# Hybrid decoder step on one core: the prompt's mask and softmax division moved to TensorE, five digit counts to ScalarE

## The chip, the cores and the metric

The kernel runs on one core of a Trainium2 chip. The metric is the device time of one execution in microseconds (us). The trace is one profiled execution; the engines are named TensorE (PE; PEld is its weight load), VectorE (DVE), ScalarE (ACT), GpSimd (POOL) and SyncE (SP).

## What is computed

Two layers of a decoder trunk for 256 prompt positions and 8 sample sequences (264 columns together), in float32. Each layer is a gated feed-forward part, a mixer, and a second feed-forward part:

```python
def layer(x, ...):
    h = macaron_ffn(x, ffn1)                       # x + 0.5 * rmsnorm(swiglu(rmsnorm(x)))
    y, state = token_mixing(rmsnorm(h), ...)       # w_in -> [conv | pool | sparse attention] -> w_out
    h = h + rmsnorm(y)
    return macaron_ffn(h, ffn2)

def dsa_prompt(q, k, v, qi, ki, wi, pos):          # 8 heads of 64, 2 key heads, blocks of 128 queries
    sc = indexer_scores(qi, wi, ki)                # sum over 4 index heads of relu(qi . ki) * wi
    sc = where(pos_k <= pos_q, sc, -inf)
    _, sel = top_k(sc, 64)                         # the 64 best keys of each prompt query
    return softmax over sel of (q . k) / 8, times v

def dsa_sample(...):                               # the same over 1024 cached keys and the new one,
    _, sel = top_k(sc, 256)                        # the 256 best of 1025; keys and values by page table
```

## The kernel before

**Feed-forward and units.** Weights come in units of 128 x 1024 floats, loaded by SyncE into six slots of `raw`. Most units are split into a high part (`w_hi`, by ScalarE, line 380) and a rest (`w_lo`, by VectorE, line 601), and each product is three fp32r products (`three`, lines 1111 to 1113). The mixer's units 9 to 15 are used unsplit, as fp32 products of eight pieces (`whole`, line 1219).

**The mixer, first stretch.** The input projection has 15 units (`unit`, then `whole`). VectorE scales each and turns queries and keys (`turned`, `rope_end`). The prompt's 64 best keys are found by eight rounds of `top8` (line 757): MAX8 and MATCH_REPLACE8 on `wk1` (256 columns) and `wk0` (128), which write TAKEN over what was found. Three rounds stand before the key unit, one after it, two after count 6 and two after count 7. The samples' 256th score is found as eight digits of a threshold: `count(i)` compares Z (16 trial values times 8 sequences on 128 partitions, 1025 columns) with the trial value and sums the flags (line 792), tests the sum against the rank (line 793), and signals `count`; TensorE sums the tests over the partitions of a sequence (`digit`, line 1237) into PSUM bank 6; `digit(i)` on VectorE makes the next trial value (lines 807 to 811). TensorE's order is: digit 0, unit 11, digit 1, unit 12, digit 2, unit 13, digit 3, unit 14, digit 4, `taps(0, 2)`, digit 5, `taps(2, 3)`, digit 6, `taps(5, 3)`, digit 7. The taps are the convolution: 496 matmul instructions of 32 x 32 weights per layer (line 1249) into banks 3, 4, 5 and 7.

**Second stretch.** ScalarE copies the taps' sums to `cpart` (line 497), TensorE folds them (line 1260). The sample keys (`keys(0)`, `keys(1)`, line 1363) use four slots of `kv`; the second batch of 32 transfers is issued by SyncE (line 264) when `keys(0)` has freed them. The prompt's attention runs over four pairs of heads j, with two buffers. `scores(j)` (lines 1377, 1378) writes banks 2 and 3; `masked(j)` on VectorE adds the mask into `sp_` (line 923), takes the maximum of each half (lines 925, 926) and scales it (line 928); `exps(j)` on ScalarE makes four exponentials with sums (line 510); `norm(j)` on VectorE takes the reciprocal (line 932) and multiplies `sp_` (line 935); TensorE transposes both halves, one into bank 7 and one into bank 0 (line 1419); ScalarE copies them to `pT` (line 528); TensorE multiplies by the values (lines 1435, 1436), ScalarE and VectorE split the result (lines 541, 956). In ScalarE's order `exps(j+1)` stands before the copies of pair j. In TensorE's order the loop body is: both transposes of j, `scores(j+2)` (for j < 2) or `keys(1)` (j = 2) or `new_key` (j = 3), values of j. The convolution's centring and variance use bank 6. After the loop the samples' mask, maximum and exponential follow (lines 1026 to 1030, 544).

**Third stretch.** TensorE transposes the samples' probabilities (line 1451), multiplies by the cached values (`values`, line 1481), does two output pieces (`out_part(1)`, `out_part(2)`), transposes the sample result (line 1491), multiplies the pool's averages (line 1495), and then waits for their split (lines 557, 1054) before the other output pieces (lines 1111 to 1113).

The order of each engine is the order in which its block is written; semaphores tie the engines together.

## Time and profile before

| | us |
|---|---|
| three runs | 1138.27, 1145.15, 1140.99 (median 1140.99) |
| profiled execution: its own time | 1138.1 |
| its span (first to last instruction) | 1136.4 |
| mixer of layer 0, from first unit to output projection | about 212 to 350 |
| mixer of layer 1 | about 770 to 908 |
| mean granted TensorE clock | 0.988 |

The page gives the busy time of each engine. The chain of work that ended last follows releases back from the end; each of its rows is a start, a duration and what ran. A timeline row has start, duration, engine, line, operation, output <- input with shapes, the number of instructions merged into it, and in brackets how long the engine had been idle and what ended that. An fp32 product appears as two instructions.

### The profile page before, as it was taken

What the parts mean: (1) busy time and instruction counts of PE and PEld (TensorE: products, weight loads), DVE (VectorE), ACT (ScalarE), POOL (GpSimd) and SP (SyncE); (2) the same over time, 40 slices, a digit from 0 to 9 for tenths busy, and PEclk for the clock granted to TensorE, in tenths of its full rate; (3) what the DMA queues carried; (4) which work ended last, traced back from release to release, by engine and by line L of the source; (5) the groups of instructions that cost most, each with busy time, mean ns of one, the idle gap of its engine ahead of it and who ended that gap; (6) DMA issues with size and microseconds to landing.
All of it is one profiled execution on the core that took longest, in us unless ns stands there. A gap on an engine that the chain in (4) does not pass through costs nothing.

```text
span 1136.4 us, 27658 instructions
## 1 busy us (share of the span) xinstructions
PE 1078.3 (95%) x9374; PEld 1024.2 (90%) x9374; DVE 740.0 (65%) x1211; ACT 513.5 (45%) x830; POOL 190.0 (17%) x241
## 2 busy tenths in 40 slices
PE   6999999999779999999999999999987899999996
PEld 5999999988459999999999999998873799999995
DVE  5667744688975766764476666448889466777544
ACT  5544443631454644443464444345216455444432
POOL 4211100411311311110042111004212022111001
PEclk9999999999899999999999999999998999999998
DMA  8464565443536455555435465563345445555541
GB/s 282 163 229 150 220 210 195 162 142 107 152 97 203 134 183 183 185 185 178 155 112 193 176 232 179 198 245 122 114 139 143 100 154 190 179 181 184 185 148 39
DMA packets 90464, 191.17 MB, mean 168 GB/s; under 512 B 12322, under 2 KB 48482, under 8 KB 90402
## 3 DMA queue, kind: packets, MB, share of 16 engines
q1 hardware_dynamic: 87426, 184.82, 48.7%
q0 software_dynamic: 2976, 5.53, 2.1%
q8 instruction: 38, 0.62, 0.2%
q14 instruction: 24, 0.20, 0.1%
HBM read 187.71 MB, written 2.59 MB: 167 GB/s over the span
## 4 chain that ended last, share of the span: by engine, by line
PE 85%; DVE 6%; ACT 4%; issue 2%; SPq 1%; DMA 1%; POOL 0%; DVEq 0%; POOLq 0%; ACTq 0%
PE PS L1111 24%; PE PS L1112 23%; PE PS L1113 23%; PE PS L1219 4%; PE PS L1147 2%; PE PS L1249 2%; DVE w_lo L601 1%; SPq L264 1%; PE PS L1158 1%; PE PS L1159 1%; PE PS L1162 1%; DVE rstd_post L630 1%; ACT w_hi L380 1%; PE PS L1225 1%; PE PS L1481 1%
## 5 line engine op out<-in xcount | busy, mean ns | idle before, releaser
L601 DVE TENSOR_TENSOR w_lo<-raw,w_hi 128x1024 fp32r<-128x1024 f32 x295 | 394.6, 1338 | 307.9 <-ACT w_hi L380 305.4
L380 ACT ACTIVATE w_hi<-raw 128x1024 fp32r<-128x1024 f32 x295 | 310.7, 1055 | 250.7 <-PE PS L1113 209.9
L1111 PE MATMUL PS<-x_hi,w_hi 128*128 128x264 f32 x1456 | 415.7, 286 | 0.7 <-DVE w_lo L601 0.6
L1112 PE MATMUL PS<-x_lo,w_hi 128*128 128x264 f32 x1456 | 412.6, 283 | 0.0
L1113 PE MATMUL PS<-x_hi,w_lo 128*128 128x264 f32 x1456 | 412.3, 283 | 0.0
L1111 PEld LDWEIGHTS PS<-x_hi,w_hi 128*128 128x128 f32 x1456 | 274.2, 188 | 2.3 <-DVE w_lo L601 1.6
L1112 PEld LDWEIGHTS PS<-x_lo,w_hi 128*128 128x128 f32 x1456 | 274.4, 188 | 0.1
L1113 PEld LDWEIGHTS PS<-x_hi,w_lo 128*128 128x128 f32 x1456 | 273.0, 188 | 0.0
L1111 PE MATMUL PS<-h_hi,w_hi 128*128 (+1 forms) x832 | 237.2, 285 | 3.7 <-DVE h_lo L1054 3.7
L1113 PE MATMUL PS<-h_hi,w_lo 128*128 (+1 forms) x832 | 236.9, 285 | 0.0
L1112 PE MATMUL PS<-h_lo,w_hi 128*128 (+1 forms) x832 | 236.2, 284 | 0.0
L1111 PEld LDWEIGHTS PS<-h_hi,w_hi 128*128 128x128 f32 x832 | 156.5, 188 | 5.0 <-DVE h_lo L1054 4.6
L1112 PEld LDWEIGHTS PS<-h_lo,w_hi 128*128 128x128 f32 x832 | 157.0, 189 | 0.0
L1113 PEld LDWEIGHTS PS<-h_hi,w_lo 128*128 128x128 f32 x832 | 156.6, 188 | 0.0
L1524 POOL TENSOR_TENSOR us<-gs,us 128x264 f32<-128x264 f32 x88 | 79.9, 908 | 431.0 <-DVE us L665 401.3
L427 ACT ACTIVATE gs<-gs 128x264 f32<-128x264 f32 x88 | 37.3, 424 | 194.2 <-DVE gs L659 194.2
L1537 POOL TENSOR_TENSOR h<-h,y 128x264 f32<-128x264 f32 x45 | 38.8, 893 | 328.4 <-DVE y L645 260.4
L1219 PE MATMUL PS<-x_all,raw 128*128 128x264 f32 x192 | 45.4, 389 | 0.0
L659 DVE TENSOR_TENSOR gs<-PS,rstd 128x264 f32<-128x264 f32 x88 | 37.9, 430 | 9.4 <-PE PS L1113 5.7
L1147 PE MATMUL PS<-sq,con 128*128 128x264 f32 x96 | 30.6, 402 | 11.9 <-ACT sq L579 10.2
L1219 PEld LDWEIGHTS PS<-x_all,raw 128*128 128x128 f32 x192 | 35.7, 190 | 5.6
L673 DVE TENSOR_TENSOR h_lo<-us,h_hi 128x264 f32 x88 | 37.5, 426 | 0.0
(255 smaller groups left out, 994.8 us busy)
## 6 DMA issues: line engine op xcount, KB each, us to landing
raw<-in_wts SPq DMA_DIRECT2D x312, 512.0 KB, 3.7
kv<-in_kT SPq DMA_DIRECT2D x128, 64.0 KB, 2.0
kx<-in_kxT SPq DMA_DIRECT2D x128, 32.0 KB, 2.1
vx<-in_vC POOLq DMA_DIRECT2D x48, 64.0 KB, 2.3
raw<-in_vC SPq DMA_DIRECT2D x32, 64.0 KB, 2.3
kv<-in_vC SPq DMA_DIRECT2D x32, 64.0 KB, 2.0
out_yT<-h SPq DMA_DIRECT2D x8, 132.0 KB, 1.8
vx<-in_vC SPq DMA_DIRECT2D x16, 64.0 KB, 1.8
```

What stands on the lines that cost most here:

```text
L380: act.activation(w_hi[:, u % SPLIT, :], raw[:, u % RAW, :], ACT.Copy) \
L427: act.activation(gs[:, f % 3, :], gs[:, f % 3, :], ACT.Silu).then_inc(sem["silu"], 1)
L601: tt(w_lo[:, u % SPLIT, :], raw[:, u % RAW, :], w_hi[:, u % SPLIT, :].bitcast(F32), AL.subtract) \
L659: tt(gs[:, f % 3, :], PS[:, 2 * (f % 3), 0:NT], rstd[:, :], AL.mult).then_inc(sem["gs"], 1)
L673: tt(out, us[:, f % 3, :], hi.bitcast(F32), AL.subtract).then_inc(sem["h_lo"], 1)
L1111: pe.matmul(out, w_hi[:, w, cols], hi, start=start, stop=False)
L1112: pe.matmul(out, w_hi[:, w, cols], lo, start=False, stop=False)
L1113: return pe.matmul(out, w_lo[:, w, cols], hi, start=False, stop=stop)
L1147: pe.matmul(PS[:, 7, 0:NT], ones, sq[:, ORDER[i], :], start=(i == 0), stop=(i == KD - 1)).then_inc(sem["mm_pre"], 1)
L1219: ins = pe.matmul(PS[:, m % 2, 0:NT], raw[:, (u0 + m) % RAW, col(k)], x_all[:, k, :], start=(k == 0), stop=(k == KD - 1))
L1524: pool.tensor_tensor(us[:, f % 3, :], gs[:, f % 3, :], us[:, f % 3, :], AL.mult).then_inc(sem["mid"], 1)
L1537: pool.tensor_tensor(h[:, d, :], h[:, d, :], y[:, d, :], AL.add).then_inc(sem["h_new"], 1)
```

## The change

- `scores(j)` first writes a mask into PSUM: `hide` (minus 1e30 on the diagonal, fp32r) times `bias` (0, 1 or 2 per query and key), one product of 384 columns for each half; the score products accumulate on it. Even pairs use banks 2 and 3, odd pairs banks 6 and 7. TensorE now waits for the mask (`mask_p`) before `scores(0)`, and for `p_exp(j-1)` before `scores(2)` and `scores(3)`.
- `masked(j)` on VectorE only takes the two maxima, from PSUM, and scales them. `exps(j)` reads PSUM and writes `sp_`.
- `norm(j)` makes `share`: the identity times the reciprocals, 128 x 4 x 128; the transposes of a half become fp32 products with `share`. Both halves use bank 0, so the second waits for ScalarE's copy of the first. The freed bank 7 and bank 6 go to the scores; fold, centring and variance move to bank 1, and the values of pair 0 wait for `c_rms`.
- Digits 0 to 4: VectorE only compares; ScalarE sums 1025 flags with an accumulating copy and tests the sum with two Relu operations on one column, each behind a semaphore wait on the one before.
- TensorE's digits 0 to 3 stand in the middle of units 11 to 14, digit 4 after `taps(0, 2)`, digit 5 after `taps(2, 3)`, and digits 6 and 7 after `taps(5, 3)`.
- Three rounds of `top8` move ahead, behind counts 0, 1 and 2; one stays behind count 6, none behind count 7.
- ScalarE's splits of units 16 to 18 stand around the sum of count 4.
- In the third stretch the pool's product and the small transposes come before `out_part(1)` and `out_part(2)`.

```diff
@@ -169,6 +172,7 @@
         ties = place("ties", [128, NS], F32, [s2[0]])
+        share = place("share", [128, 4, 128], F32, [s2[0] + 4128])
         relu = place("relu", [128, 4, 256], F32, s2)
@@ -188,7 +192,7 @@
         radi = place("radi", [128, 4 + len(SHIFTS)], I32)
-        bias = place("bias", [128, 384], F32)
+        bias = place("bias", [128, 384], F32R)
         bias1, bias0 = bias[:, 0:256], bias[:, 256:384]
@@ -212,6 +216,7 @@
         spread = place("spread", [128, 128], F32)
+        hide = place("hide", [128, 128], F32R)
@@ -235,6 +240,7 @@
         CONV_BANKS = (3, 4, 5, 7)
+        SCORES = (2, 6)
@@ -479,13 +485,31 @@
+                def summed(i):
+                    act.wait_ge(sem["beyond"], at_layer(L, "beyond", i + 1))
+                    act.activation(ties[:, :], ties[:, :], ACT.Copy, accum_out=rad[:, 6:7]).then_inc(sem["total"], 1)
+                    act.wait_ge(sem["total"], at_layer(L, "total", 2 * i + 1))
+                    act.activation(rad[:, 7:8], rad[:, 6:7], ACT.Relu, scale=-1.0, bias=rad[:, 3:4]) \
+                        .then_inc(sem["total"], 1)
+                    act.wait_ge(sem["total"], at_layer(L, "total", 2 * i + 2))
+                    act.activation(rad[:, 1:2], rad[:, 7:8], ACT.Relu, scale=-1.0, bias=con[:, C_ONE:C_ONE + 1]) \
+                        .then_inc(sem["count"], 1)
+                summed(0)
                 act.wait_ge(sem["conv_r"], at_layer(L, "conv_r", 1))
...
                 ins.then_inc(sem["conv_s"], 1)
-                for m in range(16, 19):
-                    split(L, u0 + m)
+                summed(1)
+                summed(2)
+                summed(3)
+                split(L, u0 + 16)
+                summed(4)
+                split(L, u0 + 17)
+                split(L, u0 + 18)
@@ -498,16 +522,18 @@
                 for c in range(2):
-                    ins = act.activation(cacc[:, c, 0:NP], PS[:, 7, NP * c:NP * c + NP], ACT.Identity,
+                    ins = act.activation(cacc[:, c, 0:NP], PS[:, 1, NP * c:NP * c + NP], ACT.Identity,
                                          bias=pars[:, DWB + c:DWB + c + 1])
...
                     act.wait_ge(sem["s_masked"], at_layer(L, "s_masked", j + 1))
+                    if j >= 2:
+                        act.wait_ge(sem["p_t"], at_layer(L, "p_t", 2 * j - 2))
                     for a in range(2):
                         for b, (lo, hi) in enumerate(((0, 256), (256, 384))):
-                            t = sp_[:, j % 2, a, lo:hi]
-                            ins = act.activation(t, t, ACT.Exp, scale=SCALE,
+                            ins = act.activation(sp_[:, j % 2, a, lo:hi], PS[:, SCORES[j % 2] + a, lo:hi], ACT.Exp,
+                                                 scale=SCALE,
                                                  bias=spm[:, j % 2, 2 * a + b:2 * a + b + 1],
@@ -789,8 +815,11 @@
                     at_least = trial if i else radi[:, 0:1]
-                    linked(ts(ties[:, :], Z[:, :], at_least.bitcast(F32), 0.0, AL.is_ge, AL.add, accum_out=cnt))
-                    tt(reach, cnt, rank, AL.is_ge).then_inc(sem["count"], 1)
+                    if i < SUMMED:
+                        ts(ties[:, :], Z[:, :], at_least.bitcast(F32), None, AL.is_ge).then_inc(sem["beyond"], 1)
+                    else:
+                        linked(ts(ties[:, :], Z[:, :], at_least.bitcast(F32), 0.0, AL.is_ge, AL.add, accum_out=cnt))
+                        tt(reach, cnt, rank, AL.is_ge).then_inc(sem["count"], 1)
                     if i == len(SHIFTS) - 1:
@@ -873,14 +902,17 @@
                 p0 = count(0)
+                top8()
                 turned(10, aq[:, 1, :])
                 p1 = count(1)
+                top8()
                 turned(11, aq[:, 2, :])
                 p2 = count(2)
+                top8()
                 turned(12, aq[:, 3, :])
@@ -905,23 +937,15 @@
                 top8()
-                top8()
                 p7 = count(7)
-                top8()
-                top8()
                 stt(bias1[:, :], wk1[:, :], TAKEN / 2, nc01[:, 0:256], AL.is_gt, AL.add)
-                after(L, step(L, stt(bias0[:, :], wk0[:, :], TAKEN / 2, nc01[:, 256:384], AL.is_gt, AL.add)))
+                stt(bias0[:, :], wk0[:, :], TAKEN / 2, nc01[:, 256:384], AL.is_gt, AL.add).then_inc(sem["mask_p"], 1)
                     dve.wait_ge(sem["s_p"], at_layer(L, "s_p", j + 1))
-                    if j >= 2:
-                        dve.wait_ge(sem["p_t"], at_layer(L, "p_t", 2 * j - 2))
-                    s = sp_[:, j % 2, :, :]
-                    linked(stt(s, bias[:, :].unsqueeze(1).to_broadcast([128, 2, 384]), -BIG, PS[:, 2:4, 0:384],
-                               AL.mult, AL.add))
+                    s = PS[:, SCORES[j % 2]:SCORES[j % 2] + 2, :]
                     dve.tensor_reduce(spm[:, j % 2, 0:4:2], s[:, :, 0:256], AX.X, AL.max)
@@ -930,10 +954,11 @@
                     after(L, step(L, dve.reciprocal(sps[:, j % 2, :], sps[:, j % 2, :])))
-                    for b, (lo, hi) in enumerate(((0, 256), (256, 384))):
-                        t = sp_[:, j % 2, :, lo:hi]
-                        ins = tt(t, t, sps[:, j % 2, b:4:2].unsqueeze(2).to_broadcast([128, 2, hi - lo]), AL.mult)
-                    ins.then_inc(sem["p_norm"], 1)
+                    if j:
+                        dve.wait_ge(sem["p_t"], at_layer(L, "p_t", 2 * j))
+                    tt(share[:, :, :], ident.unsqueeze(1).to_broadcast([128, 4, 128]),
+                       sps[:, j % 2, :].unsqueeze(2).to_broadcast([128, 4, 128]), AL.mult).then_inc(sem["p_norm"], 1)
@@ -1210,12 +1236,14 @@
-                def whole(m):
+                def whole(m, middle=None):
...
                     for k in range(KD):
+                        if k == KD // 2 and middle is not None:
+                            digit(middle)
                         ins = pe.matmul(PS[:, m % 2, 0:NT], raw[:, (u0 + m) % RAW, col(k)], x_all[:, k, :],
@@ -1326,26 +1354,22 @@
                 pe.wait_ge(sem["v_nat"], at_layer(L, "v_nat", 1))
-                digit(0)
-                whole(11)
+                whole(11, middle=0)
                 pe.wait_ge(sem["rope"], at_layer(L, "rope", 5))
                 turned(10)
-                digit(1)
-                whole(12)
+                whole(12, middle=1)
                 pe.wait_ge(sem["rope"], at_layer(L, "rope", 6))
                 turned(11)
-                digit(2)
-                whole(13)
+                whole(13, middle=2)
                 pe.wait_ge(sem["rope"], at_layer(L, "rope", 7))
                 turned(12)
-                digit(3)
-                whole(14)
+                whole(14, middle=3)
+                taps(0, 2)
                 digit(4)
-                taps(0, 2)
+                taps(2, 3)
                 digit(5)
-                taps(2, 3)
+                taps(5, 3)
                 digit(6)
-                taps(5, 3)
                 digit(7)
@@ -1369,20 +1393,26 @@
                         pe.wait_ge(sem["rope"], at_layer(L, "rope", 8))
+                        pe.wait_ge(sem["mask_p"], at_layer(L, "mask_p", 1))
                         pe.wait_ge(sem["c_part"], at_layer(L, "c_part", 1))
+                    elif j == 1:
+                        pe.wait_ge(sem["s_masked"], at_layer(L, "s_masked", 1))
+                        pe.wait_ge(sem["c_part"], at_layer(L, "c_part", 4))
+                        pe.wait_ge(sem["v_nat"], at_layer(L, "v_nat", 1))
                     else:
-                        pe.wait_ge(sem["s_masked"], at_layer(L, "s_masked", j))
+                        pe.wait_ge(sem["p_exp"], at_layer(L, "p_exp", j - 1))
                     for a in range(2):
                         rows = slice(64 * a, 64 * a + 64)
-                        pe.matmul(PS[:, 2 + a, 0:256], aq[rows, j, 128:256], ak[rows, 0:256], start=True, stop=True)
-                        ins = pe.matmul(PS[:, 2 + a, 256:384], aq[rows, j, 0:128], ak[rows, 0:128],
-                                        start=True, stop=True)
+                        out = PS[:, SCORES[j % 2] + a, 0:384]
+                        pe.matmul(out, hide[:, :], bias[:, :], start=True, stop=False)
+                        pe.matmul(out[:, 0:256], aq[rows, j, 128:256], ak[rows, 0:256], start=False, stop=False)
+                        ins = pe.matmul(out[:, 256:384], aq[rows, j, 0:128], ak[rows, 0:128], start=False, stop=True)
                     ins.then_inc(sem["s_p"], 1)
...
                     for c in range(2):
-                        ins = pe.matmul(PS[:, 6, 0:NT], ones, t[:, c, :], start=(c == 0), stop=(c == 1))
+                        ins = pe.matmul(PS[:, 1, 0:NT], ones, t[:, c, :], start=(c == 0), stop=(c == 1))
                     ins.then_inc(sem[name], 1)
@@ -1399,24 +1429,19 @@
                 pe.wait_ge(sem["conv_s"], at_layer(L, "conv_s", 1))
-                pe.wait_ge(sem["v_nat"], at_layer(L, "v_nat", 1))
                 channel_sum(cacc, "c_sum")
...
                     for a in range(2):
-                        if j:
-                            pe.wait_ge(sem["p_tc"], at_layer(L, "p_tc", 2 * j - 1 + a))
-                        elif a == 0:
-                            pe.wait_ge(sem["conv_p"], at_layer(L, "conv_p", 1))
+                        if j or a:
+                            pe.wait_ge(sem["p_tc"], at_layer(L, "p_tc", 2 * j + a))
                         else:
                             pe.wait_ge(sem["chunk"], at_layer(L, "chunk", 15))
-                        p = sp_[:, j % 2, a, :]
                         for n, c in enumerate((256, 0, 128)):
-                            ins = pe.transpose(PS[:, (7, 0)[a], 128 * n:128 * n + 128], p[:, c:c + 128], ident)
+                            ins = pe.matmul(PS[:, 0, 128 * n:128 * n + 128], sp_[:, j % 2, a, c:c + 128],
+                                            share[:, 2 * a + c // 256, :], start=True, stop=True)
                         ins.then_inc(sem["p_t"], 1)
@@ -1484,16 +1511,16 @@
                 values(1)
-                out_part(1, (0, 1))
-                out_part(2, (0, 1))
+                pe.wait_ge(sem["pool_y"], at_layer(L, "pool_y", 1))
+                for c in range(2):
+                    ins = pe.matmul(PS[:, 4 + c, 0:NT], raw[:, w, col(4 + c)], pw[:, c, :], start=True, stop=True)
+                ins.then_inc(sem["unit_done"], 1)
                 pe.wait_ge(sem["o_sc"], at_layer(L, "o_sc", 1))
                 ins.then_inc(sem["o_st"], 1)
-                pe.wait_ge(sem["pool_y"], at_layer(L, "pool_y", 1))
-                for c in range(2):
-                    ins = pe.matmul(PS[:, 4 + c, 0:NT], raw[:, w, col(4 + c)], pw[:, c, :], start=True, stop=True)
-                ins.then_inc(sem["unit_done"], 1)
+                out_part(1, (0, 1))
+                out_part(2, (0, 1))
```

Left out of the diff: the new semaphores' counts, and the same renaming of bank 6 or 7 to bank 1 in the fold, the centring, the channel sums and the square root.

## Rows read from the trace of the kernel before

**Rows 1.** The page, part 1: busy time and share of each engine.

```profile
PE 1078.3 (95%) x9374; PEld 1024.2 (90%) x9374; DVE 740.0 (65%) x1211; ACT 513.5 (45%) x830; POOL 190.0 (17%) x241
```

**Rows 2.** Layer 0, taps: chain that ended last (start, us, what); timeline (start, us)

```profile
272.45 3.67 PE PS L1219 x16
...
276.68 3.67 PE PS L1219 x16
...
280.34 0.12 PE PS L1237 x2
...
280.46 2.69 PE PS L1249 x115
...
287.66 0.31 PE PS L1237 x2
...
289.76 4.07 PE L1249 MATMUL PS<-gp,dgw 32*32 32x256 f32 x128 [1.78 <-issue]
```

**Rows 3.** Same chain, second stretch of the mixer, layer 0

```profile
295.42 2.07 ACT cpart L497 x4
...
298.61 1.72 PE PS L1363 x16
...
301.24 0.97 DVE sp__109 L923
...
326.48 1.14 ACT psm L544 x2
```

**Rows 4.** Same chain, and timeline of VectorE, output stretch, layer 0

```profile
331.44 3.63 PE PS L1481 x128
...
332.76 0.71 DVE L1004 TENSOR_TENSOR pw<-pw,xp 128x528 f32<-128x528 f32 x1
...
336.95 0.91 PE PS L1495 x4
...
339.71 0.39 PE PS L1111
```

**Rows 5.** Timeline of SyncE and TensorE around the second keys, both layers.

```profile
300.33 17.22 SPq L264 DMA_DIRECT2D kv<-in_kT  x32
...
319.11 1.92 PE L1363 MATMUL PS<-kv,LA 128*32 128x512 f32 x16 [1.81 <-DMA kv<-in_kT]
...
877.16 3.64 PE L1363 MATMUL PS<-kv,LA 128*32 128x512 f32 x16 [1.98 <-DMA kv<-in_kT]
```

**Rows 6.** Timeline of VectorE, digit 6 and count 7 in layer 1.

```profile
848.88 0.16 DVE L807 TENSOR_SCALAR radi<-PS 128x1 int32<-128x1 f32 x1 [0.20 <-PE PS L1237]
...
850.59 0.16 DVE L793 TENSOR_TENSOR rad<-rad 128x1 f32<-128x1 f32 x1
```

**Rows 7.** Timeline of VectorE, a selection round and a comparison in layer 0.

```profile
287.20 0.61 DVE L760 MAX8 best<-wk 128x8 f32<-128x256 f32 x2
...
305.19 0.74 DVE L945 TENSOR_SCALAR equal<-X,rad 128x1025 f32<-128x1025 f32 x1
```

**Rows 8.** Timeline of the three engines in the attention loop of layer 0.

```profile
300.25 0.71 PE L1377 MATMUL PS<-ak,aq 64*128 64x256 f32 x4
...
302.23 0.69 DVE L925 TENSOR_REDUCE spm<-sp__109 128x2 f32<-128x512 f32 x1
...
310.08 1.28 ACT L510 ACT_TABLE_LOAD   x1
...
311.53 0.51 ACT L510 ACTIVATE sp__109<-sp__109,spm 128x256 f32<-128x256 f32 x1 [0.17 <-DVE spm L928]
...
313.30 0.84 ACT L528 ACTIVATE pT<-PS 128x384 f32<-128x384 f32 x2
...
328.70 2.00 PE L1451 MATMUL PS<-spread,psm 128*128 128x128 f32 x16
```

**Rows 9.** Busy time and granted clock (PEclk) in stretches of 2 us

```profile
core 0: us, PE busy (x) PEld busy (x) DVE busy (x) ACT busy (x) POOL busy (x), PEclk, DMA share, GB/s
...
878.00:880.00 2.00, 2.00 (x16) 0.45 (x8) 1.97 (x7) 1.97 (x4) 0.00 (x0) 0.50 0.43 123
```

More of the change, by code:

```diff
@@ L72 @@
 WARM = 9
+SUMMED = 5
 BIG = 1e30
@@ L91 @@
     pool_y=1, pl_ohi=1, pl_olo=1,
-    h_last=3, step=400,
+    h_last=3, step=400, beyond=SUMMED, total=2 * SUMMED,
 )
@@ L962, in centred @@
                     for c in range(2):
-                        ins = stt(cacc[:, c, :], PS[:, 6, 0:NT], -1.0 / 256, cacc[:, c, :], AL.mult, AL.add)
+                        ins = stt(cacc[:, c, :], PS[:, 1, 0:NT], -1.0 / 256, cacc[:, c, :], AL.mult, AL.add)
                     ins.then_inc(sem["c_cent"], 1)
@@ L1088, in _ @@
             dve.wait_ge(tables, 48)
+            ts(hide[:, :], ident, -BIG, None, AL.mult)
             ts(nc01[:, 0:256], con[:, C_CA1:C_CA1 + 256], -1 / BIG, None, AL.mult)
@@ L1259, in fold @@
                     for i in range(4):
-                        ins = pe.matmul(PS[32 * i:32 * i + 32, 7, :], stack[:, :], cpart[:, i, :],
+                        ins = pe.matmul(PS[32 * i:32 * i + 32, 1, :], stack[:, :], cpart[:, i, :],
                                         start=True, stop=True)
@@ L1431, in mixer @@
                         pe.wait_ge(sem["o_lo"], at_layer(L, "o_lo", j))
+                    else:
+                        pe.wait_ge(sem["c_rms"], at_layer(L, "c_rms", 1))
                     for a in range(2):
```

4 lines of the change are left out of this document (2 added, 2 removed).

## The prediction

> **What bounds the kernel now.** I read the page first, then the chain of work that ended last, then the timelines of the mixer of both layers. TensorE is busy 95% of the span [rows 1], and the chain of work follows it through units, taps and keys [rows 2, 3]. The feed-forward parts are not touched by the change, so only the two mixers can move the time. Each has three stretches. In the first, eight digits of a threshold are found beside four weight units and the convolution's taps; TensorE is never kept waiting by a digit there, and what stops it is an "issue" gap of 1.78 us in layer 0 [rows 2], after which 128 tap instructions take 4.07 us. In the second, from ScalarE's copies of the taps to the exponentials of the samples, TensorE is sparse and the chain hops between VectorE and ScalarE (from 295.42 to 326.48 us [rows 3]); there the mask and maximum on VectorE stand in the chain. In the third, the values and the output projection, TensorE stops once more, from 337.86 us (336.95 + 0.91) to 339.71 us [rows 4].
>
> The second stretch has another bound under the first one. After the first keys, SyncE issues 32 transfers in 17.22 us, and the second keys start only when they land: keys(0) at 298.61, keys(1) at 319.11 in layer 0, 20.5 us later [rows 3, 5], with 1.81 us of waiting for a DMA. In layer 1 keys(1) begins at 877.16. Whatever VectorE saves between the two key products is therefore capped.
>
> **Part 1: five digits summed by ScalarE, each a half step later.** A count on VectorE (compare with sum, then the test) takes 1.7 us from row to row (848.88 to 850.59, with the 0.4 us of the digit's own arithmetic in it [rows 6]). A plain comparison of the same width takes 0.74 us, the sum on ScalarE is bounded by its pass over 1025 columns at 1.14 us, and two operations on one column follow, 0.3 us each as an estimate (bounds 0.2 and 0.5) [rows 3, 7]. So the five results come about 0.8 us later than today. Their step of 4.23 us (272.45 to 276.68, a unit of 3.67 us and small products [rows 2]) is set by TensorE, and the digit now waits in the middle of the unit, 1.8 us later. VectorE has in each such step: digit 0.4, comparison 0.75, prefix 0.3, one selection round of 1.5 (0.61 us for its two MAX8 [rows 7], the rest replacement), and three passes of 264 columns for the turned query and its rope, 1.05 as an estimate from 0.97 for 768 columns [rows 3]: 4.0 of 4.23 us. It fits. I cost part 1 at nothing; its cover is TensorE's unit, and if VectorE were 0.3 us longer per step, four steps would cost 1 us a layer. ScalarE was idle then; its later splits for units 17 and 18 have several us of room.
>
> **Part 2: the last digits lose their cover.** Today digit 6 stands before the last three rounds of taps and digit 7 after them, so count 7 runs under the taps. Now digits 6 and 7 both stand behind the taps. From digit 6's product to the end of the test VectorE needs 1.87 us (848.88 to 850.75 [rows 6]), then the two mask writes over 384 columns, 0.6 us by the 0.97 for 768, and only then may scores(0) start, because the mask is now an operand of TensorE. In layer 0: taps end 295.4, VectorE starts 295.8, mask ready 298.3, scores(0) 298.4, where it starts at about 296.2 today, after the first of the four copies that begin at 295.42 [rows 3]. That is +2.2 us. Behind scores(0) on TensorE are queued the fold, keys(0) and so the whole series of 32 transfers. What hid the three late selection rounds was the same stretch of taps, so moving them gains nothing.
>
> **Part 3: scores with the mask added in PSUM.** Today a pair of scores takes 0.99 us from TensorE's start to VectorE's (300.25 to 301.24 [rows 3, 8]); the two halves use 64 rows each and partly overlap. A mask product of all 128 rows between them adds two of about 0.17 us and ends the overlap. Bounds: 1.3 us (overlap kept) and 2.2 us (none, and a switch each time); I take 1.8, near the middle, since four products of 0.32 us in sequence and two of 0.17 give 1.6 plus 0.2 of latency. A full-array product among 32-row taps costs 0.31 us where one among full-array products costs 0.12 [rows 2], so a switch of tile shape has a price. The Trainium skill, TensorEngine Tiling (Array Packing), Key Properties, says that changing the tiling mode drains TensorE; by that rule the figure would be 2.0 to 2.2 us, and the two digit rows agree with it. The fold waits today for the end of the copies, 297.49; now with 298.4 plus 1.62 us it starts at 300.0: keys(0) comes 2.46 us later, at 301.07, and with it everything behind. VectorE's masking pass (0.97 us [rows 3]) is gone; its two reductions and the scaling stay, 1.25 us (0.69 for the first, of two times 256 columns [rows 8], 0.35 for the second of half the width, 0.2 for the scaling).
>
> **Part 4: the loop over the four pairs of heads.** Time from keys(0) is called k. VectorE is relieved by 1.0 us per mask and 0.35 us per division. But its relief is soon used up: before exps(2) ScalarE loads a table from 310.08 to 311.36 and starts the exponentials at 311.53 [rows 8], so VectorE was the later one by 0.17 us. And two things grow. The three transposes of a half become three fp32 products: 16 such pieces take 2.00 us [rows 8], so 0.69 us for three plus 0.2 of latency, about double. Both halves now share PSUM bank 0, so the second half waits for ScalarE's copy (0.42 to 0.47 us) of the first, and in ScalarE's order that copy stands behind exps(j+1), 1.77 us (311.53 to 313.30 [rows 8]). Two such half products, one copy and one longer pair of scores stand before exps(2), partly beside VectorE's and ScalarE's other work: I take 0.6 us (bounds -0.15, what the table load leaves, and +1.5), so exps(2) starts at k+13.5 (today k+12.9). Then one turn is: exponentials 1.77, copy 0.47, second half 0.7, scores 1.62 plus 0.2, maximum 1.25, hops 0.05: 6.05 us, so exps(3) starts at k+19.6, ends at 21.4, copy and second half bring keys(1) to k+22.6. That is past the transfers (20.5): the new chain replaces the DMA as the bound, and keys(1) is 2.1 us later relative to k. Behind it: keys 1.84, values 0.8, first half 0.9, copy 0.45, second half 0.7, new key 0.45 (values and new key estimated by the speed of the keys), then the sample's mask and maximum as today, which gives the sample's exponential at k+30.8. Today it is at 326.48, so k+27.9 in layer 0; in layer 1 it is k+29.3, because there keys(1) took 3.64 instead of 1.92 us, at a granted clock of 0.50 [rows 5, 9]. So +3.0 and +1.6 us.
>
> **Part 5: output pieces moved.** The values end at 335.07 (331.44 + 3.63), the pool's product of 0.91 us starts at 336.95 today and would start there [rows 4]. It comes 1.88 us earlier; the two output pieces (12 products of 0.12 us) and the small transposes fill the wait of ScalarE and VectorE, 1.8 us. TensorE resumes at 337.95 instead of 339.71: -1.7 us a layer. The pool's averages are ready at 333.47 (332.76 + 0.71 [rows 4]), 1.6 us before they would be wanted.
>
> **Part 6: the clock.** The new loop leaves TensorE idle for some 3.4 us before the second half of turn 1, 2.3 before that of turn 2, and 2.0 after digit 6. Today three gaps of 1.8 to 2.0 us give both answers: the taps after 1.78 us [rows 2] and keys(1) of layer 1 after 1.98 us ran slow, keys(1) of layer 0 after 1.81 us at full speed [rows 5, 9]. At half speed (1.2 instead of 2.4 GHz) the pieces behind those gaps cost up to 2.3, 2.5 and 3.4 us more: 0 to 8.2 us a layer. I take 2.5, since it holds in part of the cases and for part of each piece. The Trainium skill, TensorE: Matmul & The Clock Gate, Part 4: PE-mode transpose, says transposes don't count as activity for the clock. By that rule real products in their place would hold it better, and the sum would be without these 2.5. Rows here show transposes at full clock only.
>
> **Sum**, against the profiled execution (1138.1 us, span 1136.4): part 2 and 3 +2.46 twice = +4.9; part 4 +3.0 +1.6 = +4.6; part 5 -1.7 twice = -3.4; that is +6.1 with the clock held; part 6 +5: +11, so 1149. The median of the three runs (1141.0) is 2.9 us above the profiled one; on it, 1152.
>
> **Rivals.** (a) The same chain with the clock held at the second halves, through denser work: +6.1, so 1147. For it: keys(1) of layer 0. (b) The relief pays: ScalarE's copies and the shared bank turn out cheap (second half ready within 0.5 us of the first) and scores cost 1.3. Then keys(1) is again set by the transfers, at k+20.5; the samples' exponential comes 2.1 us earlier than in (a) per layer, and three scores give 1.5 more: 6.1 - 4.2 - 3.0 = -1.1, so 1140, no change. It decides when exps(2), one turn, the last exponentials, copy and second half, which I count as 22.6 us from keys(0), fall under 20.5. Against it: the program order on ScalarE. (c) The other side: the tap stretch loses its "issue" gap and the slow taps after it (1.78, and 4.07 for 128 instructions against 3.0 at the 2.69 for 115 of the earlier taps, with 0.3 more on the last 45: 3.1 us a layer [rows 2]), because digits no longer stand at the same points. With (a) that is +6.1 - 6.2, no change; with (b) it is -7, so 1134, faster. For it: the gap moved by some 30 instructions between layers; against: nothing waited for is removed there. (d) The clock falls at every gap: +6.1 + 16, so 1163. (e) Digits come late by VectorE's full step: +2 on any case.
>
> **Chances.** Forecast with part of the clock lost 0.40; (a) 0.25; (b) 0.15; (c) 0.10; (d) with (e) 0.10. About 0.5% (5.7 us) is what a measurement of this kernel can tell from no change. Slower: the forecast 0.40, half of (a) 0.12, (d) 0.10, so 0.62. Same: the rest of (a) 0.13, two thirds of (b) 0.10, half of (c) 0.05, so 0.28. Faster: 0.05 each of (b) and (c), 0.10. The range 1139 to 1162 leaves out most of (c) and the end of (d).
>
> **What would show it.** Right: a gap of about 2 us on TensorE between digits 6 and 7; keys(0) 2.5 us after its old distance from the taps; TensorE waiting for ScalarE's copy before each second half; keys(1) waiting for no DMA; TensorE resuming the output 1.7 us sooner after the values; small rows at double length where the clock is 0.5. Wrong: a wait for kv before keys(1) as today (b), a shorter tap stretch (c), or TensorE waiting in the middle of a unit for a digit (e).

## The result, and the profile after

The changed kernel takes 1169.14 us (median of four runs, 1161.18 to 1170.69) where the kernel before, on the same chip, takes 1143.07: the ratio is 1.023, with an interval of 1.019 to 1.027. It is slower by 26 us, more than twice the 11 us that were forecast, and outside the range. The profiled execution took 1170.7 us with a span of 1169.0, so 32.6 us more span than before. The mean granted clock fell from 0.988 to 0.972.

From the page: busy time of the engines, then the granted TensorE clock in the 40 slices of the span.

```profile
PE 1116.0 (95%) x9438; PEld 1048.3 (90%) x9438; DVE 724.0 (62%) x1176; ACT 529.8 (45%) x870; POOL 190.9 (16%) x241
...
PEclk9999999999779999999999999999997899999998
```

TensorE is busy 38 us longer than in [rows 1], with only 64 more instructions. The two dips, 77 and 78, are the second stretches of the two mixers.

The chain that ended last, layer 0 (start, duration, what ran), answers to [rows 3]:

```profile
296.81 0.17 DVE rad L822
296.99 0.04 issue
297.03 0.52 PE PS L1265 x2
297.55 0.14 issue
297.68 0.66 PE PS L1407
298.34 1.15 PE PS L1408 x2
...
302.11 1.86 PE PS L1288 x8
303.97 3.41 PE PS L1387 x16
307.38 0.39 PE PS L1407
307.77 0.63 PE PS L1408 x2
308.40 0.22 PE PS L1409 x2
...
326.00 1.15 PE PS L1408 x2
...
335.38 3.21 PE PS L1387 x16
...
345.15 1.14 ACT psm L570 x2
```

The digit's product (L1265) waits for VectorE's test, then comes the first pair of scores (mask L1407, scores L1408 and L1409), the fold and keys(0), and keys(1) only at 335.38. Two numbers carry the case. A score product of 256 columns takes 0.63 us at 307.77 and 1.15 us at 298.34 and 326.00. Keys take 3.41 and 3.21 us, against 1.72 in [rows 3]. The granted clock says why (stretches of 2 us: start:end, length, busy time of PE, PEld, DVE, ACT and POOL, then PEclk, DMA share, GB/s):

```profile
298.00:300.00 2.00, 2.00 (x6) 1.31 (x5) 0.01 (x1) 0.00 (x0) 0.57 (x2) 0.50 0.59 172
...
308.00:310.00 2.00, 2.00 (x10) 1.46 (x9) 0.13 (x1) 0.00 (x0) 0.82 (x2) 1.00 0.60 167
...
328.00:330.00 2.00, 2.00 (x7) 1.47 (x8) 0.20 (x1) 0.00 (x0) 0.00 (x0) 0.50 0.44 124
...
334.00:336.00 2.00, 2.00 (x10) 1.28 (x14) 0.52 (x1) 0.57 (x2) 0.00 (x0) 0.50 0.00 0
```

TensorE is busy without a gap in all four, and in three of them it runs at 1.2 GHz. I summed the time at the lower level from such rows over both mixers (a stretch at 0.75 counts as half of its length): 20.5 us before, 58.0 us after. The waits ahead of the falls are in TensorE's waits and timeline of the changed kernel (waits: line waited for, total, times, longest; timeline as before, idle time and its end in brackets):

```profile
PE PS L1443 <- ACT pT L554: 10.9, 8, 3.0
...
PE PS L1265 <- DVE rad L822: 4.1, 2, 2.0
```

```profile
297.03 0.52 PE L1265 MATMUL PS<-rad,con 128*128 128x1 f32 x2 [2.04 <-DVE rad L822]
...
313.82 1.33 PE L1443 MATMUL PS<-share,sp__110 128*128 128x128 f32 x6 [0.92 <-ACT pT L554]
...
324.21 1.47 PE L1443 MATMUL PS<-share,sp__110 128*128 128x128 f32 x6 [3.04 <-ACT pT L554]
...
347.10 0.43 PE L1476 MATMUL PS<-dg,con 128*128 128x64 f32 x2 [1.91 <-DVE dg L1062]
```

By milestones, as the sum of both layers against the profile of before. Each figure is a difference of starts in TensorE's and ScalarE's timelines. The last two columns are runs told below. (The +2.9 of the samples' values is the fall behind the last row above. The same wait of 1.91 us stood in the kernel before, and no fall followed it there.)

| stretch | forecast | changed kernel | useless products in the gaps | three edits |
|---|---|---|---|---|
| taps, first to last | 0 | -3.0 | -0.8 | -2.4 |
| taps' end to scores(0) | +4.4 | +4.5 | +4.4 | +0.6 |
| scores(0) to keys(0) | +0.5 | +6.4 | +3.8 | 0.0 |
| keys(0) to keys(1) | +4.2 | +22.0 | +9.4 | 0.0 |
| keys(1) to the samples' exponential | +0.4 | +3.4 | +0.8 | +0.8 |
| to the samples' values | 0 | +2.9 | +1.6 | 0.0 |
| values to the output's waiting product | -3.4 | -3.2 | -3.3 | -3.3 |
| clock, not placed | +5 | | | |
| sum | +11.1 | +33.0 | +15.9 | -4.3 |

### The profile page after: what moved, and what is told of

The parts are those of the page before. It is cut to its first block, busy times and chain, and to the rows that moved or that the text cites. A ratio compares the mean times of both kernels' runs of the same rounds, so it can differ in the third digit from the quotient of the medians.

```text
span 1169.0 us, 27801 instructions
## 1 busy us (share of the span) xinstructions
PE 1116.0 (95%) x9438; PEld 1048.3 (90%) x9438; DVE 724.0 (62%) x1176; ACT 529.8 (45%) x870; POOL 190.9 (16%) x241
## 4 chain that ended last, share of the span: by engine, by line
PE 87%; DVE 6%; ACT 4%; issue 2%; DMA 0%; POOL 0%; DVEq 0%; POOLq 0%; SPq 0%; ACTq 0%
PE PS L1137 23%; PE PS L1138 22%; PE PS L1139 22%; PE PS L1247 4%; PE PS L1173 2%; PE PS L1277 2%; DVE w_lo L627 1%; PE PS L1408 1%; PE PS L1387 1%; PE PS L1443 1%; PE PS L1185 1%; PE PS L1184 1%; PE PS L1188 1%; DVE rstd_post L656 1%; ACT w_hi L386 1%
```

## The experiments

The theory after the result: the chain's own growth is near the count, and the excess is TensorE at 1.2 GHz, let down by the waits that the change makes. The rival: the excess is work or order that was miscounted, and would be there at any clock. A run's ratio is to the kernel before measured beside it, in three groups of runs; its median was 1141.5, 1139.9 and 1141.3 us in them. The changed kernel has only its four runs above, beside a kernel before of 1143.1, so a difference to it is good to some 3 us.

### One cause at a time

**Taps cover the digits again.** `taps(2, 2)`, digit 5, `taps(4, 2)`, digit 6, `taps(6, 2)`, digit 7:

```diff
-                taps(2, 3)
+                taps(2, 2)
                 digit(5)
-                taps(5, 3)
+                taps(4, 2)
                 digit(6)
+                taps(6, 2)
                 digit(7)
```

> The changed kernel with two rounds of taps before each of the digits 4 to 7, so that count 7 runs under the taps again. Exposed-count theory: the 2.2 us between the end of the taps and the first scores go in each layer and nothing else, -4.4 us against the changed kernel. Clock theory: that 2 us gap is also what brings the granted clock down to 0.5 for the first scores, the fold and the first keys (from 296 to 307 us in layer 0); without it they run at full speed too, 3 to 4 us more a layer, -10 to -13 us in all. Rival: the taps are bound by TensorE's instruction supply, and a digit among them only moves a gap: under 2 us.

Measured: 1155.19 us, ratio 1.011 [1.006, 1.016], 14 us less than the changed kernel (expected at most 13), where the removed exposure accounts for 4.2. In layer 0 scores(0), fold and keys(0) run at full clock. The wait of 3.04 us in the loop is still there, and the products behind it are at half speed:

```profile
315.97 0.94 PE L1444 MATMUL PS<-share,sp__110 128*128 128x128 f32 x6 [3.04 <-ACT pT L554]
...
317.05 1.22 PE L1409 MATMUL PS<-ak,aq 64*128 64x256 f32 x2
```

So there are at least two falls with causes of their own, one of them behind the wait in the loop.

**Nothing removed, only TensorE kept busy.** Products of 248 columns that nobody reads, into the waits:

```diff
+                def fill(bank, n):
+                    for _ in range(n):
+                        pe.matmul(PS[:, bank, 0:248], ones, con[:, C_COS:C_COS + 248], start=True, stop=True)
...
                 digit(6)
+                pe.wait_ge(sem["chunk"], at_layer(L, "chunk", 15))
+                fill(0, 4)
                 digit(7)
...
+                pe.wait_ge(sem["p_exp"], at_layer(L, "p_exp", 1))
+                fill(2, 2)
                 for j in range(4):
...
+                        if a:
+                            fill(SCORES[j % 2], (1, 6, 2, 1)[j])
```

> The changed kernel with products of no use put into TensorE's gaps: four of 248 columns (0.41 us each at full clock) between digits 6 and 7, two before the first half products, one, six, two and one between the halves of pairs 0 to 3. Clock theory (half speed after the gaps makes up well over half of the loss): the granted clock stays at 1.0 from the taps to the output projection, keys(1) follows keys(0) by about 22 to 24 us instead of 31.5, and the time falls by 12 to 20 us. Rival (waits and order make the loss, the clock little): no change, or up to 4 us slower by the added products.

Measured: 1153.01 us, ratio 1.009 [1.006, 1.011], 16 us less than the changed kernel, with more work in the program. Keys(0) of layer 0, and the second half of pair 1, in its timeline:

```profile
302.37 2.99 PE L1393 MATMUL PS<-kv,LA 128*32 128x512 f32 x16
...
317.36 2.67 PE L1270 MATMUL PS<-con 128*128 128x248 f32 x12
320.56 0.94 PE L1453 MATMUL PS<-share,sp__110 128*128 128x128 f32 x6 [0.53 <-ACT pT L554]
...
321.60 0.70 PE L1414 MATMUL PS<-ak,aq 64*128 64x256 f32 x2
```

Counted from the start of the first half, the second half comes no earlier for this (3.98 us against 3.97); the same score products behind it take 0.70 instead of 1.22 us. The time at the lower clock falls from 58.0 to 13.7 us. This is the run that separates clock from chain: with the same order and more work, 16 us go with the clock. It is a lower bound, since 13.7 us at 1.2 GHz are left. What remains over the kernel before, 10 to 12 us, I put down to the chain. Two things missed the expectation. Keys(1) came 25.7 and 25.1 us after keys(0), not 22 to 24. And the clock did fall behind the filled wait, in both layers, from 301.6 us in layer 0 (keys(0) above takes 2.99 us), where no wait since the filled one was over 0.3 us. A wait is therefore not the whole condition of a fall.

**Both masks first, then the four scores.**

```diff
                     for a in range(2):
+                        pe.matmul(PS[:, SCORES[j % 2] + a, 0:384], hide[:, :], bias[:, :], start=True, stop=False)
+                    for a in range(2):
                         rows = slice(64 * a, 64 * a + 64)
                         out = PS[:, SCORES[j % 2] + a, 0:384]
-                        pe.matmul(out, hide[:, :], bias[:, :], start=True, stop=False)
```

> The changed kernel with both mask products of a pair first and then the four score products, so the 64-row halves stand next to each other again. Shape theory: a 256-column product took 0.63 us behind the mask where 0.43 are its columns, so each change of shape costs about 0.2 us and the halves cannot overlap; a pair of scores falls from 2.5 to about 1.4 us at full clock and from 4.2 to 2.6 at half, three such pairs on the path, -6 to -10 us over both layers. Rival (each product simply takes its columns, the order of shapes is free): no change, within 1 us.

Measured: 1150.04 us, ratio 1.007 [1.005, 1.010], 19 us less (expected 6 to 10). A pair of scores at full clock, from this run's chain:

```profile
302.98 0.55 PE PS L1405 x2
303.52 0.64 PE PS L1409 x4
304.16 0.26 PE PS L1410 x4
```

That is 1.45 us against 2.47 (307.38 to 309.85) in the changed kernel. Here four instructions, two products of 64 rows each, take 0.64 us; there two instructions, one product, take 0.63. The two halves of the array work at the same time only when their products stand next to each other, as in [rows 8]. The mask product between them had ended that: of the 1.02 us a pair, 0.8 are the scores, and 0.2 the two masks, 0.55 instead of 0.76 us. Keys(1) comes 23.1 us after keys(0) in both layers, with the 3.04 us wait unchanged. The gain is more than twice the 8 us of the shorter pairs (eight of 1.0 us), and the rest I put down to the clock: the time at the lower clock is 20.4 us.

**ScalarE's first copy of pairs 1 and 2 ahead of the next exponentials.**

```diff
                     elif j < 3:
+                        turned_copy(j, 0)
                         exps(j + 1)
+                        turned_copy(j, 1)
```

> The changed kernel with ScalarE's copy of the first half of pairs 1 and 2 moved ahead of the next pair's exponentials. Order theory (one bank for both halves, and the copy queued behind 1.7 us of exponentials and a table load of 1.3): TensorE's wait of 3.0 us before the second half of pair 1 falls to about 0.6, the wait before that of pair 2 stays near 0.5, -4 to -7 us over both layers; clock theory adds the half speed of the pieces behind that wait, another -3 to -5. Rival (VectorE or the exponentials set the turn anyway): within 1 us.

Measured: 1148.57 us, ratio 1.005 [1.002, 1.007], 20.6 us less (expected 7 to 12). The wait of 3.04 us is now 0.58. The fall behind digit 7 stays (0.50 until 306 us), the one at 324 to 338 us is gone:

```profile
321.03 0.94 PE L1448 MATMUL PS<-share,sp__110 128*128 128x128 f32 x6 [0.58 <-ACT pT L546]
...
322.07 0.70 PE L1413 MATMUL PS<-ak,aq 64*128 64x256 f32 x2
```

The four gains add up to 70 us where only 26 were lost. The time at the lower clock is 27.2, 13.7, 20.4 and 20.4 us in the four, after 58.0: each edit gives back much of the same time, so none of them can be priced alone.

### The parts of the change

**Third stretch alone**, on the kernel before: pool's product and small transposes ahead of the two output pieces.

> The kernel before with only the third stretch reordered: the pool's product and the small transposes before out_part(1) and out_part(2). My count (-1.7 us a layer, measured -1.6 in the changed kernel's trace): 3.2 us less than before, about 1138 beside a kernel before of 1141, ratio 0.997, with TensorE resuming the output 5.9 to 6.1 us after the first values instead of 8.3. The rival, that the clock or ScalarE and VectorE take the gain back later: within 0.5 us of before.

Measured: 1138.40 us, ratio 0.998 [0.996, 0.9999]. The row that waited in [rows 4] comes 6.65 us after the values in both layers, 8.31 before, and has waited 0.22 us. (The expectation's 5.9 to 6.1 us was missed. The first output piece, which waits for nothing, comes after 4.7 us.) So -3.3 us in the trace, -1.5 us between the medians, and a gain just at the edge of what the runs can tell.

```profile
338.35 0.39 PE L1111 MATMUL PS<-h_hi,w_hi 128*128 128x264 f32 x1 [0.22 <-DVE h_lo L1054]
```

**Digits' part alone**, on the kernel before: ScalarE's sums and the new places of digits and selection rounds, in the form of the change.

> The kernel before with only the digits' part of the change: ScalarE sums the flags of digits 0 to 4, TensorE's digits and the selection rounds stand where the change puts them; mask, division and third stretch as before. TensorE again waits about 2 us after digit 6, but scores(0) waits for no mask, so it follows digit 7 at once and only VectorE's masking comes later. By row lengths: +2.1 us a layer, at most 4 us in all, 1143 to 1145. If the wait after digit 6 alone brings the clock down over scores, fold and keys(0), up to 1150. If the digits' part is no loss by itself, it is within 1 us of before.

Measured: 1148.52 us, ratio 1.004 [1.001, 1.007], the second case of the expectation. Scores(0) starts 2.8 us after the taps here too, because digit 7 stands ahead of it in TensorE's order, and behind that wait the clock falls without any mask product:

```profile
296.83 0.58 PE L1260 MATMUL PS<-rad,con 128*128 128x1 f32 x2 [2.04 <-DVE rad L814]
297.35 1.23 PE L1396 MATMUL PS<-ak,aq 64*128 64x256 f32 x4
...
300.64 3.04 PE L1382 MATMUL PS<-kv,LA 128*32 128x512 f32 x16
...
322.01 1.92 PE L1382 MATMUL PS<-kv,LA 128*32 128x512 f32 x16 [2.10 <-DMA kv<-in_kT]
```

The four score instructions take 1.23 instead of 0.71 us and keys 3.04. Keys(1) is bound by the transfers again.

**Everything but the digits' part.** `SUMMED = 0`, digits and selection rounds as before; mask, division and third stretch as changed.

> The changed kernel with its digits' part undone: VectorE sums all flags, the digits stand in TensorE's order where they stood before, the selection rounds too. Mask, division and third stretch are as changed. Digit 7's count runs under the taps again, so scores(0) starts about 0.8 to 1.5 us after the taps' end (the mask writes after it), not 3.0. By row lengths alone it is 4.4 us faster than the changed kernel (1165); if the half-clock stretch starts with the wait of 2.04 us after digit 6, then scores and keys(0) run at full clock and it is 12 to 18 us faster (1151 to 1157). In both cases it stays slower than before by 8 us or more, because the turn of the loop (ScalarE's copy behind the exponentials, then the second half) is as changed. If it is equal to before, the mask and division on TensorE are no loss by themselves and the digits' part is all of it.

Measured: 1161.65 us, ratio 1.018 [1.015, 1.020]. This lies between the two forecasts and meets neither. In layer 0 digit 7 is covered and the fall at scores(0) comes later and is shorter. In layer 1 the taps took 12.7 us instead of 14.3, VectorE was still in the two late selection rounds, and TensorE waited for the mask, longer than for any digit:

```profile
867.84 0.41 PE L1405 MATMUL PS<-bias,hide 128*128 128x384 f32 x1 [2.48 <-DVE bias L938]
```

So the new wait for the mask is as good at stopping TensorE as the digit's. The loop keeps its turn in both layers: 47.8 us at the lower clock. Mask and division in the form of the change cost 23 us (this run against the third stretch alone), the digits' part 5 (by the ratio of that run alone) to 7 (by the medians), and the third stretch gives 2 to 3 back: 25 to 28 us, about the whole of the loss.

### Edits together

**Taps, masks and copy, all three** on the changed kernel.

> The changed kernel with three edits at once: taps in four parts of two rounds with digits 4 to 7 between them, both mask products ahead of the four score products, and ScalarE's first copy of pairs 1 and 2 ahead of the next exponentials. Alone they took 14, 19 and 20.6 us off. If each had its own loss, the sum would be 54 us, below any floor; the theory that all three removed the same stretch at half clock expects the clock at 0.99 and counts what is left by row lengths: digit 7 one digit after taps (+0.8 us instead of +3.0), pair of scores 1.45, turn about 6.5, keys(1) at k+21 to k+22, samples' exponential at k+29.5, third stretch -2.3: within 3 us of the kernel before, 1138 to 1144, ratio 0.998 to 1.003. If a loss independent of the clock hides in the mask and division on TensorE, it stays over 1147.

Measured: 1134.33 us, ratio 0.994 [0.992, 0.996]: 35 us less than the changed kernel, and faster than the kernel before. The time at the lower clock is 3.4 us in both mixers together. The chain is as short as before, and the transfers bound keys(1) again:

```profile
296.46 0.59 PE L1411 MATMUL PS<-bias,hide 128*128 128x384 f32 x2 [0.47 <-ACT cpart L521]
...
298.72 1.90 PE L1393 MATMUL PS<-kv,LA 128*32 128x512 f32 x16
...
319.40 1.92 PE L1393 MATMUL PS<-kv,LA 128*32 128x512 f32 x16 [1.08 <-DMA kv<-in_kT]
```

I had expected 1138 to 1144. The keys were expected at k+21 to k+22 and came at k+20.7, and the clock held better than before.

**The same with useless products in the loop**, `fill` with (1, 3, 2, 1).

> The three edits of the run before and useless products into TensorE's waits of the attention loop (none after digit 6, whose wait is gone). If half-clock stretches are left in the second stretch with the three edits, this one is 2 to 6 us faster than that; if the three edits already hold the clock as before, it is equal to it or up to 3 us slower, because a useless product started just ahead of a release delays it by up to 0.5 us.

Measured: 1136.21 us, ratio 0.996 [0.994, 0.998]. Nothing is left for them to hold, as the second case of the expectation has it.

**Masks and copy, taps as changed.**

> The changed kernel with both mask products ahead of the scores and ScalarE's first copy ahead of the exponentials; the taps and digits stay as changed. Alone the two edits took 19 and 20.6 us off and left 20 us at half clock each. Theory that they removed the same stretch: together they leave at most 14 us at half clock and the wait after digit 6 (2.2 us a layer): 1141 to 1146, 3 to 8 us over the version with the taps' edit too. If their gains added up, the time would be under 1134.

Measured: 1142.76 us, ratio 1.001 [0.998, 1.003]. The two edits to the loop take off 26 us together, not 40: they had removed the same time at the lower clock, of which 20.5 us are left, as after either edit alone (the expectation had at most 14). The difference to the version with all three, 8 us, is the place of digit 7: its wait of 2.04 us is still there, and 0.50 until 302 us.

**Masks and copy, with VectorE summing all digits**: `SUMMED = 0` as above.

> The same two edits on the version in which VectorE sums all flags: mask and division on TensorE in their better order, the digits as before, the third stretch as changed. It tells what ScalarE's sums bring. If they bring nothing beyond what digit order and taps settle, this is equal within 3 us to the version with all three edits (1134). VectorE has the last two selection rounds and the mask writes after count 7 here, so scores(0) comes 0.4 to 2.0 us later per layer than there: I expect 1135 to 1140.

Measured: 1139.73 us, ratio 0.997 [0.994, 1.000]. In layer 0 scores(0) follows the taps after 0.87 us, in layer 1 after 3.06 us, again behind the mask of the late selection rounds. Against the version with all three edits this is 5 us more between the medians, with intervals that overlap. So ScalarE's sums seem to bring what they make room for: selection rounds moved out of the way of a mask that TensorE now waits for.

**The digits' part with the taps' edit and the third stretch; VectorE masks and divides.**

> The kernel before with the digits' part, the taps in four parts of two rounds with digits 4 to 7 between them, and the third stretch as changed, but VectorE masking and dividing as before. If mask and division on TensorE bring nothing even in their better order, this equals the version with all three edits: 1134 to 1137. By my count the second keys stay bound by the transfers in both (k+20.6), and the samples' exponential follows 7.3 us after them here against 8.4 there: 1 us a layer better, 1132 to 1137.

Measured: 1136.87 us, ratio 0.996 [0.994, 0.999], with an interval that overlaps the 0.994 of all three edits. Mask and division on TensorE, even in their better order, bring nothing that these runs can tell. In the traces the two are 3.7 us apart, and 3.0 of them lie in the taps, not in the loop (see rival (c) below).

## Why the prediction was wrong

**Part 1, sums on ScalarE at nothing: right.** Steps stayed at 4.23 us and TensorE waited for no digit in the middle of a unit, so (e) didn't happen.

**Part 2, the two late digits, +2.2 us a layer: the time was right and the consequence was priced too low.** 3.01 us from taps to scores(0) in both layers against 0.78 before. But the 2.0 us of waiting that I named under the clock lie directly ahead of scores(0), fold and keys(0), and I gave all that stands behind them 3.4 us at most, and took a third of that. In layer 0 they cost some 4.4 us more than at full clock. The row with 0.50 and keys at 3.41 us show it, and the digits' part alone shows it without mask or loop.

**Part 3, a pair of scores at 1.8 us: mis-sized.** It is 2.47 us at full clock, over my upper bound of 2.2. The step that failed is "four products of 0.32 us in sequence and two of 0.17". The 0.32 comes from halving the row of [rows 8], but its four instructions are two products running at once, so one alone takes the whole 0.63; the four score products take 1.70 us, not 1.28. A mask product takes 0.37 to 0.39 us, not 0.17. Each of the two errors is 0.4 us a pair. With eight pairs in two layers they are 5 to 7 us. The Trainium skill, TensorEngine Tiling (Array Packing), Key Properties, says that a change of mode drains TensorE, and I counted such drains up to the 2.2. The runs show that the order mask, mask, scores costs 1.45 us with the same instructions and fewer changes. The 0.8 us of the scores is the lost overlap; a drain can be no more than part of the other 0.2.

**Part 4, the loop: the mechanism was right, and its time too where the clock held.** With masks first, exps(2) starts 13.1 us after keys(0), whose start is k (forecast 13.5), keys(1) at k+23.1 (22.6), and the second half of pair 1 waits for ScalarE's copy, by 3.04 us (forecast 3.4). In the changed kernel it was k+31.4, and with useless products k+25.1 and k+25.7. That 23.1 is so near 22.6 is in part luck, since the pairs there take 1.45 us where the sum had 1.62, and one term was missing: in ScalarE's order the split of a pair's values also stands ahead of the exponentials, and those values stand behind the next scores on TensorE. That made ScalarE wait 5.10 us until 331.31 in layer 0. At full clock it costs little, since VectorE's maximum comes at the same time.

**Part 5, -1.7 us a layer: right**, 1.6.

**Part 6, the clock, +5: this is where the forecast failed.** It is at least 16 us by the run with useless products. I had bounded it at 8.2 us a layer by the pieces directly behind three gaps, two in the loop and one after digit 6, and then taken a third of that. In layer 0 the rows at the lower level are scores(0) and scores(3) (+2.0, +1.6 us over 2.47), fold (+0.8), keys(0) and keys(1) (+1.7, +1.4), three half products (1.33, 1.47 and 1.65 us instead of 0.94) and the samples' transposes (2.84 against 2.00 in [rows 8]): 10 us in one layer, and every one of them is on the chain. The chain hands it on: a slower half product makes the next copy later, and the next wait longer. Case (d), the clock falling at every gap, was the nearest; 1163 and the 5 to 7 us of part 3 make 1168 to 1170, in part by luck, since the taps' -3.0 us is in the measured time and not in that sum. I gave it a tenth, because three gaps of before had given both answers. That weighing rested on a misread row. Keys(1) of layer 1 ran slow, but the clock had been at 1.2 GHz since 874 us, ahead of the 1.98 us of waiting that ended at 877.16. And it left out the two longest waits for other engines in the loop of before, 2.37 and 1.85 us in each layer: the clock fell at all four, at the latest 1.5 us behind their end. Timeline of before, and the stretch in which the clock fell in layer 1:

```profile
304.64 1.54 PE L1419 MATMUL PS<-con,sp__109 128*128 128x128 f32 x6 [2.37 <-DVE sp__109 L935]
...
872.77 0.76 PE L1435 MATMUL PS<-pT,vn 128*64 128x256 f32 x4 [1.85 <-DVE h_lo L956]
...
874.00:876.00 2.00, 1.19 (x6) 0.79 (x6) 1.93 (x5) 0.18 (x1) 0.00 (x0) 0.56 0.44 120
```

But for keys(1) of layer 1 those falls cost little, because the work behind them was mostly off the chain or followed by a wait that absorbed it (1.8 us before keys(1) of layer 0). The change took that cushion away too: there is no wait for a DMA ahead of keys(1) any more.

The Trainium skill, TensorE: Matmul & The Clock Gate, Part 4: PE-mode transpose, says that transposes don't count as activity for the clock, and I drew from it a sum without the clock's term, since real products replace transposes. The trace speaks against that use of it: with real products in their place the loop fell to 1.2 GHz. My sentence that the rows show transposes at full clock only holds for the rows quoted: the transposes at 304.64 above ran at 1.2 GHz for the most part (1.54 us, where 0.87 is full speed). No run here tests the rule itself.

**Rival (c), shorter taps:** it came by half, -3.0 us in the trace. In layer 1 the tap stretch takes 12.0 to 13.8 us in all ten kernels that mask and divide on TensorE, and 14.5 to 16.3 us in the four that don't; TensorE's "issue" gaps before taps add up to 2.1 to 4.0 us in the ten and 4.8 to 5.1 in the four. Layer 0 shows no such difference (14.3 to 14.9 and 13.8 to 15.1 us). So it goes with the mask and division, though the digits' places don't bring it, and why is open.

What stays open is when the clock falls and how long a fall lasts. The wait of 1.91 us before the samples' transposes is in every kernel and layer, and a fall followed it in 12 of 28 cases; the wait of 3.04 us was followed by one in all eight, of 3.4 to 13.7 us. With masks first it was shorter behind the same wait (0.50 until 301 us instead of 306). The copy's edit left the first one as long as it was in layer 0. There is one profile for each kernel, so part of such differences may be chance.

## What to carry to other kernels

Price a wait on the bottleneck engine twice: once for its length, and once for the case that the clock falls, for the work behind it at 1.2 GHz, along the chain, until something absorbs it. Here a wait of 2.0 us and one of 3.0 us cost more through the second price than through the first. Before you divide the time of a merged row by its count, ask whether its instructions ran side by side; a product of another shape put between two that share the array costs the overlap. And if useless products in a gap win time, the gap is to be removed: reordering the same instructions gave 35 us, filling the gaps 16.

## What the hardware showed that was not expected

- The score products of two halves side by side cost 0.90 us (0.64 + 0.26), those of one half alone 0.85 us (0.63 + 0.22); with a 128-row mask product between the halves a pair takes 2.47 instead of 1.45 us.
- TensorE can be busy throughout and stay at half speed for long: 298 to 306 us and 326 to 332 us in layer 0, in rows with 2.00 us busy of 2.00.
- A wait of 2.04 us before a product of one column was followed by the lower clock in both layers of all five kernels that had it and put nothing into it (two of them: 296.83 and 297.03 us above). With useless products in that wait the clock still fell in both layers, but for 3.4 us each instead of 10.3 and 6.8.
